# Inverses of the first block's two lanes: the forward lane is given its levels ahead of the backward lane's last row steps

## The reference, cut to what matters

```python
t_mat = a_mat + jnp.eye(GDN_CHUNK)            # a_mat strictly lower triangular
rhs = jnp.concatenate([v * beta[..., None], k_beta * jnp.exp(g)[..., None]], axis=-1)
sol = lax.linalg.triangular_solve(t_mat, rhs, left_side=True, lower=True, unit_diagonal=True)
...
o_fwd = gated_delta_rule_chunked(qg, kg, vg, g_f, beta_f)
o_bwd = flip(gated_delta_rule_chunked(flip(qg), flip(kg), flip(vg), flip(g_b), flip(beta_b)))
```

## Time and profile before

| | us |
|---|---|
| median of three runs | 2878.84 |
| lowest and highest | 2876.41, 2880.3 |
| profiled execution | 2878.79 |
| its span, first to last instruction | 2877.0 |
| TensorE busy | 2626.2 (91% of the span) |
| VectorE, ScalarE, GpSimd busy | 982.3, 723.9, 605.7 |

### The profile page before, as it was taken

How to read it: one execution, slowest core, us unless ns; L and a number is a source line. 1 busy time by engine, 2 the same in 40 slices (tenths; PEclk the granted TensorE clock), 3 DMA queues, 4 the chain that set the end, 5 groups by cost and what they waited for, 6 DMA issues and landing times.

```text
span 2877.0 us, 34074 instructions
## 1 busy us (share of the span) xinstructions
PE 2626.2 (91%) x14331; PEld 1711.4 (59%) x14331; DVE 982.3 (34%) x1724; ACT 723.9 (25%) x1218; POOL 605.7 (21%) x185
## 2 busy tenths in 40 slices
PE   8999979879999999888988898888889899999998
PEld 7766767777657643333323333256667766788886
DVE  3257856753121311011011110133494522360332
ACT  3257633523112110000100100033442212421212
POOL 3300644623113000000000000031121122344342
PEclk9999979979999999999999999999999999999999
DMA  4301113104225799999999999953010033333231
GB/s 162 117 16 60 61 57 118 59 2 146 84 78 204 285 406 428 428 428 428 428 428 429 428 428 429 427 208 121 30 33 16 14 112 103 110 97 101 90 101 73
DMA packets 131044, 559.36 MB, mean 194 GB/s; under 512 B 7320, under 2 KB 88672, under 8 KB 103272
## 3 DMA queue, kind: packets, MB, share of 16 engines
q1 hardware_dynamic: 130056, 551.28, 48.7%
q0 software_dynamic: 864, 6.29, 0.6%
HBM read 547.01 MB, written 10.54 MB: 194 GB/s over the span
## 4 chain that ended last, share of the span: by engine, by line
PE 71%; DMA 13%; DVE 9%; ACT 4%; issue 2%; POOL 1%; DVEq 0%; SPq 0%; ACTq 0%; POOLq 0%
DMA S<-in_w_up 11%; PE PS L612 8%; PE PS L614 8%; PE PS L613 8%; PE PS L2216 7%; PE PS L2183 7%; PE PS L602 4%; PE PS L2166 2%; PE PS L3435 2%; PE PS L3437 2%; PE PS L3438 2%; PE PS L3273 2%; PE PS L2227 1%; DMA S<-in_w_down 1%; PE PS L633 1%
## 5 line engine op out<-in xcount | busy, mean ns | idle before, releaser
L2183 PE MATMUL PS<-S 128*64 128x512 f32 x2048 | 457.1, 596 | 72.5 <-DMA S<-in_w_up 67.9
L612 PE MATMUL PS<-r_block,r_block 128*128 128x512 f32 x1040 | 419.0, 403 | 7.1 <-POOL r_block L2539 5.2
L613 PE MATMUL PS<-r_block,r_block 128*128 128x512 f32 x1040 | 405.9, 390 | 0.0
L614 PE MATMUL PS<-r_block,r_block 128*128 128x512 f32 x1008 | 393.6, 390 | 0.0
L2183 PEld LDWEIGHTS PS<-S 128*64 128x64 f32 x2048 | 140.8, 137 | 379.5 <-issue 247.1
L2539 POOL TENSOR_TENSOR r_block<-S,r_block 128x2048 fp32r<-128x2048 f32 x55 | 257.9, 4690 | 484.5 <-ACT r_block L2527 475.8
L492 POOL TENSOR_TENSOR r_block<-S,r_block 128x2048 fp32r<-128x2048 f32 x40 | 183.3, 4582 | 551.0 <-ACT r_block L484 329.4
L2216 PE MATMUL PS<-S 128*64 128x512 f32 x1024 | 225.6, 597 | 6.2 <-DMA S<-in_w_down 3.0
L612 PEld LDWEIGHTS PS<-r_block,r_block 128*128 128x128 f32 x1040 | 195.8, 188 | 56.3 <-issue 10.9
L613 PEld LDWEIGHTS PS<-r_block,r_block 128*128 128x128 f32 x1040 | 196.0, 188 | 44.9 <-issue 5.8
L2412 POOL TENSOR_TENSOR S<-S 128x1024 f32<-128x1024 f32 x4 | 9.5, 2390 | 973.5 <-DVE S L2400 973.5
(11 more groups left out here) (491 smaller groups left out, 3758.7 us busy)
## 6 DMA issues: line engine op xcount, KB each, us to landing
S<-in_w_gate SPq DMA_DIRECT2D x64, 2048.0 KB, 18.0
S<-in_w_up SPq DMA_DIRECT2D x64, 2048.0 KB, 21.0
S<-in_w_down SPq DMA_DIRECT2D x64, 2048.0 KB, 25.6
S<-in_w_in SPq DMA_DIRECT2D x57, 1024.0 KB, 5.3
S<-in_w_up SPq DMA_DIRECT2D x16, 1024.0 KB, 5.5
S<-in_w_down SPq DMA_DIRECT2D x16, 1024.0 KB, 4.9
S<-decay_rows SPq DMA_DIRECT2D x8, 1024.0 KB, 7.1
S<-in_w_out SPq DMA_DIRECT2D x8, 1024.0 KB, 5.2
```

What stands on the lines that cost most here:

```text
L612: pe.matmul(out, wh, r32(HT[:, dc, :]), start=(dc == 0), stop=False)
L613: pe.matmul(out, wh, r32(low[:, dc, :]), start=False, stop=False)
L614: mm = pe.matmul(out, wl, r32(HT[:, dc, :]), start=False, stop=(dc == DC - 1))
L2183: mm = pe.matmul(PS[c * CAP:(c + 1) * CAP, 2 + 2 * m + g, :], XE[:, 2 * q + r, e * CAP:(e + 1) * CAP], w[:, r, 1024 * g + 512 * c:1024 * g ...
```

## The change

Only the order is changed, in the three functions, and for both groups: no instruction is added or taken away, save that u6 and x6 are issued for one lane after the other in place of both in turn. Lane b's row tasks come three behind lane f's in place of two. Lane f's u4, x4 and u5 are put between lane b's last row tasks, and from there on lane f is half a level ahead.

```diff
@@ heads_pe
-            for p in range(7 + 2):
-                if p < 8:
-                    inv_rows_pe(pe, f, gr, sel, p)
-                if p >= 2:
-                    inv_rows_pe(pe, b, gr, sel, p - 2)
+            for p in range(8):
+                inv_rows_pe(pe, f, gr, sel, p)
+                if p >= 3:
+                    inv_rows_pe(pe, b, gr, sel, p - 3)
             inv_u4_pe(pe, f, gr)
+            inv_rows_pe(pe, b, gr, sel, 5)
+            inv_rows_pe(pe, b, gr, sel, 6)
+            inv_x4_pe(pe, f, gr)
             inv_rows_pe(pe, b, gr, sel, 7)
+            inv_u5_pe(pe, f, gr)
             inv_u4_pe(pe, b, gr)
-            inv_x4_pe(pe, f, gr)
+            inv_x5_pe(pe, f, gr)
             inv_x4_pe(pe, b, gr)
-            inv_u5_pe(pe, f, gr)
+            inv_u6_pe(pe, [f], gr)
             inv_u5_pe(pe, b, gr)
-            inv_x5_pe(pe, f, gr)
+            inv_x6_pe(pe, [f], gr)
             inv_x5_pe(pe, b, gr)
-            inv_u6_pe(pe, LANES, gr)
-            inv_x6_pe(pe, LANES, gr)
+            inv_u6_pe(pe, [b], gr)
+            inv_x6_pe(pe, [b], gr)
@@ heads_act
             inv_u4_act(act, f, gr)
+            inv_u5_act(act, f, gr)
             inv_u4_act(act, b, gr)
-            inv_u5_act(act, f, gr)
             inv_diag_act(act, f, gr)
+            inv_u6_act(act, f, gr)
             inv_u5_act(act, b, gr)
             inv_diag_act(act, b, gr)
-            inv_u6_act(act, f, gr)
             inv_u6_act(act, b, gr)
@@ heads_dve
-            for i in range(15 + 5):
-                if i == 5:
+            for i in range(15):
+                inv_step_dve(dve, f, gr, i)
+                if i == 4:
                     inv_small_dve(dve, b, gr)
-                if i == 16:
-                    inv_wide_dve(dve, f, gr)
-                if i < 15:
-                    inv_step_dve(dve, f, gr, i)
                 if i >= 5:
                     inv_step_dve(dve, b, gr, i - 5)
+            inv_wide_dve(dve, f, gr)
+            inv_u4_dve(dve, f, gr)
+            inv_step_dve(dve, b, gr, 10)
+            inv_step_dve(dve, b, gr, 11)
+            inv_step_dve(dve, b, gr, 12)
+            inv_x4_dve(dve, f, gr)
+            inv_step_dve(dve, b, gr, 13)
+            inv_step_dve(dve, b, gr, 14)
             inv_wide_dve(dve, b, gr)
-            inv_u4_dve(dve, f, gr)
             inv_u4_dve(dve, b, gr)
-            inv_x4_dve(dve, f, gr)
+            inv_x5_dve(dve, f, gr)
             inv_x4_dve(dve, b, gr)
-            inv_x5_dve(dve, f, gr)
+            inv_x6_dve(dve, f, gr)
             inv_x5_dve(dve, b, gr)
-            inv_x6_dve(dve, f, gr)
             inv_x6_dve(dve, b, gr)
```

## The result

| | before | changed |
|---|---|---|
| median, us | 2878.84 (5 runs) | 2891.52 (5 runs, 2889.35 to 2894.86) |
| ratio | | 1.0047, 95% interval 1.0033 to 1.0062 |
| profiled execution, span | 2877.0 | 2888.8 |
| stretch of group 0 (first row task to last L1254) | 54.8 | 62.4 |
| stretch of group 1 | 55.5 | 60.3 |

A second set of the changed kernel, beside later experiments, gave 2889.62 us, 1.0035 (1.0022 to 1.0048). I had forecast 2878.0, and 2871 to 2883 as the range: wrong, and the chance of a loss over 0.2% was put at 0.12. The two stretches explain all of it: 7.6 + 4.8 = 12.4 us of the 11.8 that the spans differ.

The account below looks back on a forecast made before the run. It took a TensorE, VectorE and ScalarE chain with waits as the bound. 2878.79 + 0.0 (group 0) - 0.8 (group 1) gave 2878.0 us, range 2871 to 2883.

Parts of the forecast that it names:

- What bounds the stretch: Group 0's 55.0 us: a TensorE, VectorE, ScalarE chain; some 7 us of TensorE waits a lead could fill.
- Lane f's end of the row steps: Lane f's last two row-step products and transpose start 0.4 us sooner, so u4 f can start at 382.15.
- The pause and the clock ahead of u4 f: TensorE idles some four us before u4 f, so it runs at 1.2 GHz: 3.6 us, not 2.06.
- b5 and b6: Lane b's two row tasks between u4 f and x4 f: 3.5 us at half clock, where full clock would cost 1.9.
- the last level's price: Lane-by-lane u6 and x6: x6 f 1.8 us, u6 b two halves of 0.9, from 3.62 for four halves.
- GpSimd: Its clear waits some 8 us longer, its products end near 409, still hidden by the scan at 418.
- A stop without a reason: The unexplained stop within x4, 2.07 us in group 0: bounds 0 and 2.07 a group in the changed order, taken as 0.
- the second rival: TensorE fed late where small products stand on end: 7.5 us more, 2885.5; chance 10%.
- Group 1's row steps: f3 no longer queued behind b0; 1.65 us saved if the clock stays full, group 1 taken as -0.8.
- The scan's start: The scan may start at half clock: nothing or about 1.6 us a group, taken as 0.
- the first (full clock past x4): Clock stays full until lane f is past x4: 3.2 us a group sooner, 2871.6; chance 22%.
- The third: The change does not do what it says: group 1's row steps at half clock, one stop a group, 2882.2; chance 12%.

Follow-up runs that it names:

- e8: Kernel before with only the level order changed: x4 f ahead of u4 b, row tasks in place but the last, u6 and x6 interleaved; ratio 0.9961, 2869.68 us.
- e6: Kernel before with lane b's row tasks three behind lane f's in place of two, levels untouched; ratio 0.9994, 2878.64 us.
- e13: e8 with lane b's row tasks b5 and b6, and VectorE's steps 10 to 12, behind lane f's u4; ratio 1.001, 2883.77 us.
- e3: Changed kernel with eight products of 128x256 that nothing reads in TensorE's pause ahead of u4 f; ratio 1.0013, 2883.61 us.
- e12: The changed kernel itself measured again, beside e10 and e13; ratio 1.0035, 2889.62 us.
- e2: Kernel before with u6 and x6 issued one lane after the other in place of both in turn; ratio 1.0031, 2889.9 us.
- e10: e8 with the change's last level, u6 f, u5 b, x6 f, x5 b, u6 b, x6 b; ratio 1.0011, 2882.9 us.
- e11: e2 with each lane's u6 and x6 products going to its two PSUM banks in turn; ratio 1.0031, 2889.27 us.
- e1: Changed kernel with u6 and x6 of both lanes together at the end, interleaved as before; ratio 1.0028, 2887.73 us.
- e9: e8 with products that nothing reads put into its remaining waits between levels; ratio 0.9979, 2875.36 us.

## Why the prediction was wrong, step by step

- **What bounds the stretch**: right. A chain of three engines with waits to be filled; e8 fills them and gains 11 us.
- **Lane f's end of the row steps**: I had u4 f 0.4 us sooner, at +19.0. It came at +19.43, as before (+19.44). VectorE's first L1215 starts 0.7 us sooner, but takes 1.26 us in place of 0.53 and ends at +18.2 in both kernels, 0.3 behind the end of GpSimd's L1260. First the two rows before, then after:

```profile
372.12 9.01 POOL L1260 TENSOR_TENSOR S<-S 128x2048 f32<-128x2048 f32 x2
380.87 0.87 DVE L1215 TENSOR_TENSOR S<-S 128x256 f32<-128x256 f32 x2
```

```profile
370.27 8.99 POOL L1260 TENSOR_TENSOR S<-S 128x2048 f32<-128x2048 f32 x2
378.29 1.59 DVE L1215 TENSOR_TENSOR S<-S 128x256 f32<-128x256 f32 x2
```

  The same end, +18.2, stands in e6, e8 and e13. Where this operation starts behind L1260, as in group 1 before (+19.3), it takes 0.42. So a head start for lane f ahead of +18.2 is worth nothing while GpSimd is at L1260. That the two engines are in each other's way is read from these rows; no run moved L1260.
- **The pause and the clock ahead of u4 f**: right, in mechanism and size. TensorE idles, the clock is 0.50 in u4 f (3.63; I said 3.6), and e3 shows the cause, with 3.3 us for it where the sum had 3.2.
- **b5 and b6**: right, 3.7 us where I had 3.5. x4 f at +26.7 (+26.0), u4 b at +33.8 (+33.0). That the clock comes back behind them held in group 1 and not in group 0 (in e12 in both).
- **The failed step is the last level's price**: "u6 f runs under that", "x6 f 1.8", "u6 b from 413.9: a half of 0.9, another to 415.7 (3.62 for four halves, rows 3)". I divided the time of two lanes' interleaved products by two. Each of the four sets took 3.3 to 3.7, not 1.8. In group 0, which missed its +54.8 by 7.6 us, 6.3 of it are this. u6 f, which I had under VectorE's work, held u5 b back by 1.1 us (VectorE's transpose had ended at 406.2, u5 b started at 407.28). x6 f held x5 b back by 2.3 (ScalarE was through at 410.4, x5 b started at 412.72), of which 1.8 are what it took beyond the 1.8 that I gave it. And from the start of u6 b to the end it took 7.5 where I had 4.1, 3.4 more. The other 1.3 are the 0.8 by which u4 b was late and what of the stop below reached the chain. e2, e10 and e11 show the price by itself. The price stood in the trace of before, at the second block's u6.
- **GpSimd**: right. Its last product of the group ends at 408.7, 15 us ahead of the scan.
- **A stop without a reason**: I took 0; it came as 1.29 us in group 0 and 0.30 in group 1, before x4 b's last records. It is part of the miss in group 0, but not the second rival: no stop appeared in the last level, and the loss is there without one.
- **Group 1's row steps**: right (1.5 of 1.65). The -0.8 that I took for the group was lost in the rest: its stretch grew by 4.8.
- **The scan's start**: the clock is half there in the changed kernel, as I had thought possible, and its first 16 records take 3.66 us in place of 2.88. It costs nothing all the same, as I had taken it: before, the clock fell within those 16 records (my "starts at full clock" was true of their start alone) and the next set ran at half clock. In group 0 the fourth set of the scan starts 5.27 us behind the first in both kernels (423.44 - 418.17 and 429.17 - 423.90).
- **The rivals**: the first (full clock past x4) was built as e3. Its price of the clock, 6.4 us a kernel, held (6.0 between e12 and e3), but its 2871.6 rested on the wrong halves: e3 is 0.13% slower than before. The rival on the slower side had the right sign by another mechanism. The third didn't come: group 1's row steps kept full clock. No rival named the sharing of the array, which decided.

The forecast of a draw was thus a sum of a loss of 8.6 us up to lane b's u4, which came (9.3), and a gain of 8.5 behind it, which came as 1.7: from u4 b to the end it was 30.3 us before and 28.6 after, where I had 21.8. The price of the last level explains why the gain didn't come, not the loss itself: with both lanes in turn again (e1) the kernel is still 0.28% slower than before, and what is left is lane b's lateness at u4, which e13 shows on its own in part.

## What to carry to other kernels

Before a set of small products is split or moved, ask what its neighbours in the stream were: interleaved products on two parts of the array may take no longer than one part's alone, and half the set is then not half the time. Look for a place in the same trace where the smaller set already runs alone. And a lead for one lane is worth having only where the last lane's chain isn't touched: take it from waits, not from the other lane's work, and check what the engine that is now idle does to its clock.

## What the runs showed of the hardware that was not expected

- Products of 64x64 on one part of the array: 0.105 us a record at 1.2 GHz (6.72 / 64, e2), 0.065 at 2.4 (2.08 / 32, before); two parts in turn: 0.057 and 0.032. PSUM banks in turn change nothing (e11).
- x4's set of 128 records takes 1.90 us at half clock and 1.26 at full (e3); the forecast had taken it as equal for want of a row.
- x4 b's stop before its last records returned in the changed kernel (1.29 and 0.30 us) and within x5 in others (0.91 in e8's x5 f, 1.11 in e9's), within u4 or u5 now and then (0.66 in e8's u4 b of group 1), though the order around it differed. The transfer of instructions is the candidate, and the traces speak for it: taken together, the 14 have 30 stops of 0.3 to 2.2 us without a semaphore between u4 f and x6, and each of them ends 2.2 to 2.8 us after a transfer of 16 KB on the queue of instructions (q8) began. Such transfers come 3 to 10 us apart there, so that chance would put few stops at such a distance. Many transfers have no stop behind them, and nothing was built to test it, so the cause is not shown.
- VectorE's first L1215 ends at +18.2, 0.3 us behind GpSimd's L1260, whether it started at +17.0 or +17.7: it takes 1.26 us or 0.53, and 0.42 with L1260 out of the way.
